# The low halves of the u weights computed on POOL in two pieces, and DVE's dot products issued up to six places later

## What is computed

```
def peer(h, wq, subkeys, u, v):                      # 512 prompt rows and 32 sample rows, D = 1024
    ...
        q = (xb @ wq).reshape(PEER_BLOCK, 8, 2, 128)
        s = einsum('thpd,hpkd->thpk', q, subkeys)     # 8 heads, 2 halves, 128 keys
        s_top, i_top = top_k(s, 16)
        cand = s_top[:, :, 0, :, None] + s_top[:, :, 1, None, :]
        g_s, g_i = top_k(cand, 16)                    # 16 experts of 16384, for each row and head
        g = softmax(g_s)
        act = gelu(einsum('thed,td->the', u[e], xb))  # e: the chosen experts
        return einsum('the,thed->td', g * act, v[e])
```

## Time and profile before

| | |
|---|---|
| three runs | 2226.19, 2227.39 (median), 2228.25 us |
| the profiled execution: its time, its span | 2228.25 us, 2226.6 us |
| busy in the span | PE 91%, PEld 74%, DVE 72%, ACT 38%, POOL 26% |
| the stage that the change touches | about 955 to 1667 us |
| mean granted PE clock | 0.954 of full speed |

### The profile page before, as it was taken

The page is one execution under the profiler, slowest core; times in us unless marked ns, Lnnn a source line. Parts: engine busy times, 40 slices in busy tenths (PEclk is TensorE's granted clock), DMA queues, the critical chain, the costliest instruction groups (busy, mean ns, idle before and its releaser), DMA issues.

```text
span 2226.6 us, 32324 instructions
## 1 busy us (share of the span) xinstructions
PE 2030.9 (91%) x10471; PEld 1637.8 (74%) x10471; DVE 1604.2 (72%) x3110; ACT 854.5 (38%) x1715; POOL 579.9 (26%) x599
## 2 busy tenths in 40 slices
PE   8998999669879999969899799979998999999997
PEld 7774576234446558869899789979997888888885
DVE  3563256775224346889999899989758999999988
ACT  1232022113202221124676476647853333333331
POOL 1000133332200000001222223223325555554540
PEclk9999899878989999989999899999999999999998
DMA  5333232997850231437799699969989999999992
GB/s 199 80 74 116 85 100 71 328 358 265 295 228 3 114 105 57 130 105 235 246 315 304 231 295 323 307 227 330 369 313 395 394 403 392 396 389 397 383 391 94
DMA packets 239937, 547.81 MB, mean 246 GB/s; under 512 B 22190, under 2 KB 122335, under 8 KB 238394
## 3 DMA queue, kind: packets, MB, share of 16 engines
q1 hardware_dynamic: 110714, 287.40, 36.7%
q0 software_dynamic: 60736, 208.40, 25.5%
q10 hardware_dynamic: 68352, 50.34, 6.9%
HBM read 485.58 MB, written 60.02 MB: 245 GB/s over the span
## 4 chain that ended last, share of the span: by engine, by line
PE 34%; DVE 18%; issue 6%; ACT 3%; DMA 2%; ACTq 0%; SPq 0%; DVEq 0%; POOLq 0%
PE psum L2805 22%; PE psum L2559 7%; DVE u_gather L2457 4%; PE psum L2116 3%; DVE hT L2485 2%; PE psum L2575 1%; DVE uL L2231 1%; DVE eq L2027 1%; ACT hT L2420 1%; DVE eq L2024 1%; DMA S<-activation_table 1%; DVE vecs L2028 1%; ACT uH L2363 1%; DVE cand L1989 1%; ACT hT L2415 1%
## 5 line engine op out<-in xcount | busy, mean ns | idle before, releaser
L2221 POOL DMA_INDIRECT u_gather<-in_u_rows,gather_ids x160 | 186.7, 1167 | 847.2 <-DVE dots L2457 497.2
L2559 PE MATMUL psum<-hH,uH 128*128 128x384 f32 x1024 | 354.3, 346 | 49.2 <-DVE uL L2231 49.2
L2559 PE MATMUL psum<-hH,uL 128*128 128x384 f32 x1024 | 346.4, 338 | 0.0
L2559 PE MATMUL psum<-hL,uH 128*128 128x384 f32 x1024 | 346.2, 338 | 0.0
L2805 PE MATMUL psum<-vH,wH 128*128 128x512 f32 x768 | 302.0, 393 | 11.3 <-DVE wL L2749 11.3
L2805 PE MATMUL psum<-vH,wL 128*128 128x512 f32 x768 | 300.9, 392 | 0.0
L2667 POOL DMA_INDIRECT v_gather<-in_v_rows,idx_now x160 | 236.9, 1481 | 245.8 <-DVE y_sample L2756 146.6
L2805 PE MATMUL psum<-vL,wH 128*128 128x512 f32 x768 | 300.7, 392 | 0.0
L2559 PEld LDWEIGHTS psum<-hH,uH 128*128 128x128 f32 x1024 | 195.3, 191 | 52.8 <-DVE uL L2231 52.4
L2457 DVE CUSTOM_DVE_ANT_0 u_gather<-u_gather,h 128x1024 f32<-128x1024 f32 x160 | 195.4, 1221 | 4.0
L2559 PEld LDWEIGHTS psum<-hL,uH 128*128 128x128 f32 x1024 | 195.7, 191 | 0.0
(11 more groups left out here) (510 smaller groups left out, 3331.5 us busy)
## 6 DMA issues: line engine op xcount, KB each, us to landing
u_raw<-in_uT SPq DMA_DIRECT2D x128, 512.0 KB, 5.3
S<-in_v_rows SPq DMA_DIRECT2D x64, 512.0 KB, 11.0
v_rest<-in_v_rows SPq DMA_DIRECT2D x64, 512.0 KB, 6.7
activation_table<-acts ACTq DMA_DIRECT2D x128, 192.0 KB, 4.6
gate_table<-Gtile ACTq DMA_DIRECT2D x48, 512.0 KB, 7.0
S<-gate_table SPq DMA_DIRECT2D x16, 768.0 KB, 7.3
S<-activation_table SPq DMA_DIRECT2D x16, 768.0 KB, 13.4
G_rest<-gate_table SPq DMA_DIRECT2D x16, 768.0 KB, 8.2
```

Source lines behind the costliest of these rows:

```text
L2221: c.nc.gpsimd.indirect_dma_start(c.ug[:, k % RG], None, c.A["u_rows"].rearrange("j i d -> (j i) d"), bass.IndirectOffsetOnAxis(ap=c.ids[:, ...
L2559: ins = nc.tensor.matmul(column[n % 4][:, 0:ND], w[:, n % RU, d], x[:, d], start=m == 0, stop=m == len(parts) - 1)
```

## The change

`low_u` goes from DVE's list to POOL's, and becomes two instructions of four slices (128x512) each, with one count at the end; its wait for `u_mm` goes, as ACT has waited for the same count before it wrote `uH`. POOL does the first three columns right behind the first two gathers, and then column n+3 at place n, as ACT does. POOL's gather k+2 moves into the list at dot place k; before, all gathers stood in a row. DVE's list has no columns any more. At dot place k, DVE issues dots until at most DOT_LAG = 6 remain open (`while dots + DOT_LAG <= k`); before each convert in steps 3 and 7 of p = 1 and 2, before each late pick and once behind them it issues one dot ahead, if more than one place is open (`spare_dot`). What is left is issued at the end.

```
+DOT_LAG = 6
 def pool_scores(pool):
     for k in range(2):
         gather_u(c, pool, k)
+    for n in range(AHEAD):
+        pool.wait_ge(c.u_hi, n + 1)
+        low_u(c, n)
...
-def low_u(c, dve, n):
-
-    dve.wait_ge(c.u_hi, n + 1)
-    if n >= RU:
-        dve.wait_ge(c.u_mm, n - RU + 1)
-    c.nc.vector.tensor_tensor(c.uL[:, n % RU], c.u[:, n % RAW], c.uH[:, n % RU].bitcast(F32),
-                              ALU.subtract).then_inc(c.u_split, 1)
+def low_u(c, n):
+
+    for d in (slice(0, KD // 2), slice(KD // 2, KD)):
+        ins = c.nc.gpsimd.tensor_tensor(c.uL[:, n % RU, d], c.u[:, n % RAW, d],
+                                        c.uH[:, n % RU, d].bitcast(F32), ALU.subtract)
+    ins.then_inc(c.u_split, 1)
...
             def _(pool):
                 pool_scores(pool)
-                for k in range(2, NDOT):
-                    gather_u(c, pool, k)
+                def columns(n):
+                    n += AHEAD
+                    if n < NKEYS:
+                        pool.wait_ge(u_hi, n + 1)
+                        low_u(c, n)
+
+                def dot(k):
+                    if k + 2 < NDOT:
+                        gather_u(c, pool, k + 2)
+                steps(columns, dot, *[nothing] * 7)
...
                         elif st % BATCH == BATCH - 1:
+                            spare_dot()
                             router.convert(b.first, BATCH)
                             if st == PH - 1:
                                 for h in range(BATCH, PH):
+                                    spare_dot()
                                     router.pick(h, b.res)
+                                spare_dot()
...
-                def columns(n):
-                    low_u(c, dve, n)
-
-                steps(columns, dot, tile_pre, nothing, tile_gates, nothing, unit, route, nothing)
+                places = dots = 0
+
+                def next_dot():
+                    nonlocal dots
+                    dot(dots)
+                    dots += 1
+
+                def spare_dot():
+                    if dots < places - 1:
+                        next_dot()
+
+                def dots_late(k):
+                    nonlocal places
+                    places = k + 1
+                    while dots + DOT_LAG <= k:
+                        next_dot()
+
+                steps(nothing, dots_late, tile_pre, nothing, tile_gates, nothing, unit, route, nothing)
+                while dots < NDOT:
+                    next_dot()
```

More of the change, by code:

```diff
@@ L2253, in stage_activate @@
         G = c.G[:].rearrange("p (a j t) -> p a j t", a=2, t=TB)
-        c.u_mm, u_act, g_mm, g_ev = (c.sem(n) for n in ("u_mm", "u_act", "g_mm", "g_ev"))
-        u_mm = c.u_mm
+        u_mm, u_act, g_mm, g_ev = (c.sem(n) for n in ("u_mm", "u_act", "g_mm", "g_ev"))
         a_stored, G_stored = c.a_stored, [c.sem(f"G_stored{i}") for i in range(2)]
```

## The result

The changed kernel takes 2253.66 us, median of 4 runs (2245.7 to 2255.58), beside 2227.82 us for the kernel before on the same chip (4 runs, 2226.19 to 2229.51): a ratio of 1.0105, 95% interval 1.0086 to 1.0125. It is 1.05% slower, where 2194 us was predicted, and it lies outside the predicted range. The profiled execution of after took 2246.42 us, its span is 2244.7 us and its mean granted clock 0.953 (before 0.954).

A forecast was written before the change was run, and what follows sets the result against it. PE, busy 91% of the span, was taken as the bound. Gains 16.5 + 1.8 + 29.7 + 5.4 = 53.4 us, less 20 us for POOL's pieces, gave 33.4 us and 2194 us; range 2168 to 2240 us.

The forecast's parts named there:

- slower rival: SBUF read path: POOL's pieces also hold DVE's two-tensor instructions; 68 us slower, 2295 us, at 15% idle path; chance 0.22.
- DVE's relief: DVE in the stage: 35 subtractions, 42.9 us, leave its 179.91 us busy, so 137 us remain and it stops bounding.
- the price of the pieces: POOL's subtractions: 1.2 us plus 0.55 us waiting, 1.75 us each; POOL exceeds PE's steps, charging 20 us together.
- the sign turned at 53.4: Gain without any charge was 53.4 us; a larger charge from POOL's reading would make the kernel slower.
- The start: First column: PE begins at 958.6 instead of 975.07 us because POOL is idle then; 16.5 us gained.
- cold clock: PE's matmuls after long idle times run at 1.2 GHz, losing 1.8 us each; savings 1.8 us and 5.4 us.
- The turns: Changes from tile to tile: PE's remaining waits for `uL` behind DVE's queue all go; 29.7 us gained.
- waits for `hT`: PE's idle time behind the transposes, 5.16 us at the turn shown, one for each of three turns, stays.
- the ring of four: DVE's units run ahead of PE by a whole step, which covers late gathers and dots at no cost.
- The dots' moves: Dots issued later or ahead on DVE: each still costs 1.22 us, only its place moves; costed at nothing.
- The ring of `u_raw`: SP's loads of u wait for POOL's subtraction: 8.8 to 13.2 us against 14.6 us, so hidden.
- threshold of 5%: Idle share of the read path from which the charge for mutual exclusion passes 53.4 us and the change loses.

The follow-up runs named there:

- first3: Kernel before with only the first 3 columns subtracted on POOL, two pieces each, dots in their old places: 2223.77 us, ratio 0.9963.
- first16: Kernel before with the first 16 columns, up to the turn to tile 1, subtracted on POOL, dots in their old places: 2228.21 us, ratio 0.9985.
- first21: Kernel before with the first 21 columns, the whole first tile, subtracted on POOL: 2228.86 us, ratio 0.9981.
- write_only_long: Changed kernel with each POOL piece replaced by two waited-for writes of 512 elements, one into uL, one into a spare tile: 2180.52 us, ratio 0.9777.
- write_only: Changed kernel with POOL's two subtracting pieces replaced by four instructions that write zeros to uL and read nothing: 2176.24 us, ratio 0.9747.

## Why the prediction was wrong

**The mechanism was the slower rival's,** "the read path excludes both ways", to which 0.22 was given. Its marks came as they were put: DVE's dots at 1.8 us, POOL idle on dots while PE waits for POOL's `uL`. That a piece in flight holds DVE's instruction is seen in the timelines above, and the runs set the sizes: without reading on POOL 2176 and 2181 us, with the dots alone out of the exclusion 2186, with both reading 2254.

**The step that failed is DVE's relief:** "left with 137 us [...] It doesn't bound any more unless it is blocked", and with it the price of the pieces, which charged the collision to POOL alone. I had put 0.55 us of waiting on each piece. Measured, the pieces took 378.1 us, 256 undisturbed ones 321.8: 0.22 us of waiting each, 56 us in all. DVE was relieved of 142.8 us and got 188.6 us back as stretch. Likewise "Each dot costs DVE what it did, 1.22 us": it cost 1.82. Set against the two kernels in which POOL only writes (ratios 0.9747 and 0.9777 for 1.0105), the exclusion cost 73 to 80 us, where the forecast charged 20 and the sign turned at 53.4. The one row that I held against it, that no row of DVE is stretched beside a gather, was weak: a gather of 0.94 us reads one list of indices, and no row of before had POOL read two tensors.

**The price of a piece by itself was right:** 1.257 us at least and 1.302 in the median, for 1.2. The estimate worked out from the Trainium skill (GPSIMD Engine Reference, section "Performance versus the Vector engine"), 1.15 us, was below it by 0.11 us; the measured 1.257 decides.

**The start** (16.5 us) was right at its place: idle time 19.51 to 3.26, 16.25 us. 12.9 us of it were left at the first transposes. The 1.8 us of cold clock were not saved: the matmuls behind the 3.26 us of idle time begin 0.32 us apart, the same lower level as in the earlier trace rows. By itself it is worth 0.4% (first3, 8 us), less than half of what the forecast took for it; first16 and first21 have it and are faster by 0.2% at most, as DVE's routing is late for it.

**The turns** (29.7 us, and 5.4 of cold clock): PE's waits for `uL` behind the start were to be none and are 41.8 - 3.26 = 38.5 us. At the two turns shown 4.7 and 2.9 us were gained; the rest is 23 other waits, most of them short and in the steps. Of the 29.7 us only 16.8 were at these two turns to begin with. The cold clock wasn't saved either, as more of PE's work fell under the lower clock than before (44.6 us for 35.6). The waits for `hT` were to stay and went from 18.5 to 34.2 us, as DVE's units were late: the ring of four was no cover for a stretch that doesn't end.

**The dots' moves at nothing:** right where nothing collides (2176 us with the moves in it, against 2174 for the sum without charge), and a lag of three was far worse. Wrong as a general price: left with the subtractions on DVE they cost 14 us.

**The ring of `u_raw`** didn't bind: ACT waits for `u_raw` 29.2 us in all, less than the 73.3 before, and POOL's idle time is laid to dots.

**The rival's size.** It gave 2295 us, with 15% of the path idle. Counted as it was there, a step needs 12.9 us of DVE's instructions and ten pieces, now 12.6 us: 25.5. Eight are 204 us of the 219.5 that a tile took: 7% idle, just past the threshold of 5% that I had worked out, and far from 15. With 7% and the measured piece the rival's formula gives 16 x (25.5/0.93 - 24.43) + 8 x (19.9/0.93 - 18.2) = 73 us, less 53.4: 20 us slower, where the stage lost 18. This is no independent confirmation, as the 7% comes out of the measured 219.5 us. The sum agrees, its parts less so. Tile 3 was the other way round: 8 x (11.1 + 7 x 1.257) = 159 us in 191.5, a turn and a tail included; it lost most, 25.1 us, with the path idle for a sixth. There it is not the path's total that binds but who waits at the time. At the turn PE idles 11.94 us until 1503.90; DVE's timeline there:

```profile
1494.64 2.66 DVE L2002 TENSOR_TENSOR cand<-v 128x256 f32<-128x256 f32 x1
...
1499.85 0.83 DVE L2016 TENSOR_SCALAR ab<-gi_sample 128x32 uint32<-128x32 uint32 x1
...
1501.39 3.56 DVE L2495 TENSOR_TENSOR hT<-iota,bcol 128x768 f32<-128x768 f32 x4
```

The one-hot rows of the units begin at 1501.39, 9.9 us after the transposes; before it was 3.6 us. Routing in front of them took 2.9 us longer, as the candidates' sum took 2.66 us instead of 0.43 and the TENSOR_SCALAR 0.83 instead of 0.18. The rest is that DVE came to this routing only 0.5 us before the transposes, where it had come 4.0 us before. For the 18.7 us in that tile's columns I have the waits (POOL for dots, DVE for gathers), but no run that takes one away alone; how they divide stays open.

## What to carry to other kernels

Work moved from one engine to another that shares a read path isn't taken off the first: count the path's time over both, and the stretch of every two-tensor instruction that stays, before calling the first relieved. If a kernel has long stretches of such work on DVE, try a few pieces on POOL where PE is idle, above all at the start, and leave the steady stretch alone: three columns of 128 gave 0.4%, sixteen plus six with a lag of three 0.8%, all of them lost 1.05%. And an early start is a gain only when whatever ends the tile is early as well.

## What the runs showed that I had not expected

- DVE waits behind a whole train of POOL's pieces: a dot of 1.22 us that began in a gather took 4.17 us and ended only after the two pieces that followed the gather, where POOL's own waits never passed about one instruction of DVE (longest piece 2307 ns).
- It isn't only instructions with two tensors that were stretched. A CAST of 128x128 took 1350 ns on average for 0.23 us, and two TENSOR_SCALAR of 128x64 took 1.25 and 1.19 us, each until a piece of POOL ended; the reduction L2028, also one tensor, kept its 686 ns. None of the CAST and TENSOR_SCALAR of these lines took over 241 ns before. Lines of the timeline of DVE in the changed kernel:

```profile
1235.14 1.25 DVE L2016 TENSOR_SCALAR ab<-gi_first 128x64 uint32<-128x64 uint32 x1
1236.43 1.19 DVE L2017 TENSOR_SCALAR ab<-gi_first 128x64 uint32<-128x64 uint32 x1
```

  beside this of POOL:

```profile
1234.91 2.66 POOL L2233 TENSOR_TENSOR uL<-u_raw,uH 128x512 fp32r<-128x512 f32 x2
```

- Writes of POOL don't stretch the instructions with two tensors: dots 1227 ns beside 512 writes of 318 ns, and beside 512 of 0.53 us. They do stretch the CAST and TENSOR_SCALAR: to 0.68 us at most in write_only_long, and one TENSOR_SCALAR to 1.80 us in write_only. In the lines below, of write_only_long, a CAST of usually 0.23 us lasted until a write of POOL ended. DVE's comes first, then POOL's:

```profile
1207.49 0.57 DVE L2018 CAST abf<-ab 128x128 f32<-128x128 uint32 x1
```

```profile
1207.44 0.54 POOL L2234 MEMSET uL<- 128x512 f32 x1
```

- Shorter holders of the path aren't fairer in the end: 256 elements a piece relieved DVE and made POOL's column 0.9 us longer; 1024 spared POOL and put the stretch on the one-hot rows. Both cost 1.0 to 1.2% more than 512.
